# Values of a head multiplied one head later in the four short attention blocks of a hybrid decoder layer

## What is computed

```
h = rms_norm(x); proj = h @ w_in                      # q, k, v, indexer q/k/weights, four HGRN2 parts
for each block of 128 queries:                        # 16 blocks
    score = sum_h wi_h * relu(qi_h . ki)              # indexer, 8 heads of 64
    keep the 256 best causal keys of every query
    for each of 8 heads: p = softmax(q . k / 8 over kept keys); o = p @ v
hg  = gated linear recurrence (4 heads of 128)
x1  = x + rms_norm(concat(o, hg) @ w_out)
out = x1 + rms_norm((silu(n @ w_gate) * (n @ w_up)) @ w_down),  n = rms_norm(x1)
```

## Time and profile before

| | before |
|---|---|
| median of three runs | 3378.53 us |
| the profiled execution | 3383.49 us, span 3381.5 us |
| granted TensorE clock, mean | 0.983 |
| PE busy | 3214.6 us (95%) |
| DVE busy | 2267.9 us (67%) |
| ACT busy | 1501.5 us (44%) |
| DMA, mean | 102 GB/s |

### The profile page before, as it was taken

The page is one execution under the profiler, slowest core; times in us unless marked ns, Lnnn a source line. Parts: engine busy times, 40 slices in busy tenths (PEclk is TensorE's granted clock), DMA queues, the critical chain, the costliest instruction groups (busy, mean ns, idle before and its releaser), DMA issues.

```text
span 3381.5 us, 46512 instructions
## 1 busy us (share of the span) xinstructions
PE 3214.6 (95%) x18048; PEld 2836.7 (84%) x18048; DVE 2267.9 (67%) x3817; ACT 1501.5 (44%) x2477; POOL 237.1 (7%) x400
## 2 busy tenths in 40 slices
PE   8999999999888899999989999998999999989998
PEld 8999999998777788888778888887888888868886
DVE  3467777788565766666787777677876765463445
ACT  3454455445455454443554444445554444333222
POOL 0000000000111110010110001011000000010000
PEclk9999999999899999999989999999999999999999
DMA  5543443344222222222522212134111112252233
GB/s 182 168 134 121 131 149 125 114 139 130 98 84 104 94 83 80 68 85 69 180 83 76 71 63 79 64 111 150 63 65 60 64 52 74 95 182 97 91 105 107
DMA packets 147501, 345.66 MB, mean 102 GB/s; under 512 B 15057, under 2 KB 35921, under 8 KB 145233
## 3 DMA queue, kind: packets, MB, share of 16 engines
q1 hardware_dynamic: 144976, 338.49, 30.2%
q10 hardware_dynamic: 2304, 4.20, 0.3%
HBM read 283.31 MB, written 59.31 MB: 101 GB/s over the span
## 4 chain that ended last, share of the span: by engine, by line
PE 63%; DVE 5%; ACT 2%; issue 2%; DMA 1%; SPq 0%; DVEq 0%; POOL 0%; ACTq 0%; POOLq 0%
PE PJ_d L2069 9%; PE PJ_d L2071 9%; PE PJ_d L2070 9%; PE SC L2025 7%; PE PJ_d L2094 6%; PE PJ_d L2096 6%; PE PJ_d L2095 6%; PE SA L1984 3%; PE SA L2011 3%; PE SA L1985 3%; PE SA L1980 1%; DVE score L1716 1%; DVE wd_lo L1825 1%; DVE prob L1810 1%; DVE h_lo L1830 0%
## 5 line engine op out<-in xcount | busy, mean ns | idle before, releaser
L2069 PE MATMUL PJ_d<-h_hi,wd_hi 128*128 128x512 f32 (+1 forms) x1472 | 577.1, 392 | 15.4 <-DVE h_lo L1830 9.9
L2071 PE MATMUL PJ_d<-h_hi,wd_lo 128*128 128x512 f32 (+1 forms) x1472 | 564.6, 384 | 0.0
L2070 PE MATMUL PJ_d<-h_lo,wd_hi 128*128 128x512 f32 (+1 forms) x1472 | 563.8, 383 | 0.0
L1579 ACT ACTIVATE wd_hi<-wd_raw 128x512 fp32r<-128x512 f32 x568 | 345.2, 627 | 229.6 <-DMA wd_raw<-in_w_gu 128.6
L733 PE MATMUL PJ<-w_hi,h_hi 128*128 128x338 f32 (+1 forms) x1280 | 416.0, 325 | 2.8 <-DVE w_lo L550 2.8
L1825 DVE TENSOR_TENSOR wd_lo<-wd_raw,wd_hi 128x512 fp32r<-128x512 f32 x568 | 380.5, 689 | 45.9 <-ACT wd_hi L1579 42.9
L734 PE MATMUL PJ<-w_lo,h_hi 128*128 128x338 f32 (+1 forms) x1280 | 408.6, 319 | 0.0
L735 PE MATMUL PJ<-w_hi,h_lo 128*128 128x338 f32 (+1 forms) x1280 | 408.5, 319 | 0.0
L1574 ACT ACTIVATE pT<-SA 128x512 f32<-128x512 f32 (+3 forms) x320 | 156.6, 532 | 519.4 <-PE SA L2011 519.4
L1810 DVE CUSTOM_DVE_ANT_0 prob<-SA,bias 128x1024 f32<-128x1024 f32 (+7 forms) x192 | 170.1, 911 | 314.2 <-PE SA L1985 306.9
L2069 PEld LDWEIGHTS PJ_d<-h_hi,wd_hi 128*128 128x128 f32 x1472 | 280.8, 191 | 66.4 <-DVE wd_lo L1825 6.8
(11 more groups left out here) (207 smaller groups left out, 5724.6 us busy)
## 6 DMA issues: line engine op xcount, KB each, us to landing
wd_raw<-in_w_gu SPq DMA_DIRECT2D x352, 256.0 KB, 2.9
wd_raw<-in_w_down SPq DMA_DIRECT2D x176, 256.0 KB, 2.6
w_raw<-in_w_in SPq DMA_DIRECT2D x40, 684.0 KB, 4.6
w_raw<-in_w_in SPq DMA_DIRECT2D x40, 676.0 KB, 4.5
row_h<-proj_d SPq DMA_DIRECT2D x16, 1024.0 KB, 7.0
proj_d<-stage SPq DMA_DIRECT2D x40, 342.0 KB, 4.5
proj_d<-stage SPq DMA_DIRECT2D x40, 338.0 KB, 5.0
x_d<-acc SPq DMA_DIRECT2D x24, 512.0 KB, 2.9
```

The source lines that it names most:

```text
L1579: s_.activation(w_hi[:, u % RING, :], w_raw[:, u % RING, :], ACT.Copy).then_inc(w_hi_ready, 1)
L2069: t.matmul(to[:, tok], w_hi[:, r, w], h_hi[:, c, tok], start=(c == 0 and part != 1), stop=False)
L2070: t.matmul(to[:, tok], w_hi[:, r, w], h_lo[:, c, tok], start=False, stop=False)
L2071: last = t.matmul(to[:, tok], w_lo[:, r, w], h_hi[:, c, tok], start=False, stop=(c == KD - 1 and part != 0))
```

## The change

In the blocks with one chunk, PE multiplies the values of head h - 1 directly behind the turned probabilities of head h, ahead of slot B. The last head's values stay behind its slot B. In the other blocks nothing changes. Units 12 to 15, the `("out", 0, 0, 1, j)`, get the step 50 in place of 49, so that ACT rounds them in slot B of head 7 and the DVE splits them at step 51, in the index phase of block 4.

```diff
@@ -956,7 +956,8 @@
-        split_step[u] = min(max(freed + 2, split_step.get(u - 1, 0) + again), unit_first[u] - 3)
+        late = 1 if units[u][0] == "out" and units[u][1] == 0 and units[u][3] == 1 else 0
+        split_step[u] = min(max(freed + 2 + late, split_step.get(u - 1, 0) + again), unit_first[u] - 3 + late)
@@ -2122,6 +2123,14 @@
                     fill(("A", b, h))
+                    if NCH(b) == 1:
+                        turn_probs(b, h, 0)
+                        if h >= 1:
+                            values(b, h - 1, 0)
+                        fill(("B", b, h))
+                        if h == HEADS - 1:
+                            values(b, h, 0)
+                        continue
                     for p in range(pairs_of(b)):
```

## The result

The changed kernel takes 3362.9 us, the median of six runs (3360.6 to 3365.9), against 3379.3 (3376.7 to 3383.2) for the kernel before in the same job. The ratio is 0.9949, with a 95% interval of 0.9939 to 0.9959: 16.3 us less, where 19.9 were forecast. The profiled executions take 3365.1 and 3383.5 us, 18.4 apart.

The account below looks back on a forecast made before the run. PE, busy 95% of the span, was taken to bound the kernel. The terms 3.7 + 4.0 + 5.1 + 2.2 + 4.9 = 19.9 us, taken off the median of 3378.5, gave 3358.6 us; range 3353 to 3368.

Parts of the forecast that it names:

- The high ends: All parts of the change at their most favourable values: a total gain of about 24 us.
- The waits go, and PE's gain is kept: Blocks 0 to 3: waits for the copy fall from 13.0 to under 2 us; the DVE, behind PE, lets the gain stand.
- The rival that the softmax takes the copy's place: PE reaches the next turned head too soon and waits for its softmax, over 9 us in blocks 0 to 3; 3370.6; chance 0.10.
- Block 3, 3.7 us: Heads 2 to 5 of block 3: each gains 0.92 us by instruction starts, 3.7 in all; 2.8 by idle time.
- Block 2, 4.0 us: Heads 0 and 2 to 5 of block 2: five gaps of 0.80 us each go, 4.0 in all.
- Block 1, 5.1 us: Block 1: head 3 gives 3.8 us at full clock, head 4 0.3, head 6 0.7, head 7 0.3.
- the low branch: Block 1, head 3: if item 16 still runs at half clock, the gain is 1.5 us in place of 3.8.
- Block 0, 2.2 us: Block 0: 1.0 us from heads 0 to 2 and 1.2 from heads 3, 5, 6 and 7.
- Heads 0 to 2, taken as 1.0: Block 0, at half clock until about 914: gain between 0.7 and 2.3 us, taken as 1.0.
- The 1.2 us for heads 3, 5, 6 and 7: Block 0: the next softmax or an opening is close behind, so between 0 and 2.2 us, taken as 1.2.
- The split, 4.9 us: End of block 3 to item 52: head 7's softmax and item 52 come 5.0 us earlier, less 0.1 for ACT's roundings.
- Behind block 4 nothing changes: From block 4 on, all engines and loads are ahead by the same amount, and the rest takes as long as before.

Follow-up runs that it names:

- the last experiment: Against the changed kernel, the new order kept in blocks 2 and 3 alone, blocks 0 and 1 as before: 3368.9 us, ratio 0.9970.
- the second profile: Profile of the changed kernel run again with nothing changed, in a later job: 3362.3 us, ratio 0.9950.

## Why the prediction was right, and by how much not

Right were the sign, the mechanism and the range: 3362.9 against 3358.6 (3353 to 3368). The sum was 3.6 us too high, and the kernel before came out 0.7 above the median that it was taken from. The high ends as the prediction states them add up to 22.8 us, not to 24; with them the forecast's own lower bound would be 3355.7 and not 3354.5.

- **The waits go, and PE's gain is kept.** Under 2 us of waiting for the copy were forecast, 0.2 are left. The rival that the softmax takes the copy's place is refuted at its size, 4.3 us and not over 9. It is not wholly false: apart from head 7 of block 3, PE waits 2.3 us more for the softmax than before, 1.0 in block 0, 0.7 in block 1 and 0.5 in block 2.
- **Block 3, 3.7 us.** Measured 3.7, twice. Here the two ways to read the gap could be told apart: by starts 3.7, by the idle time of the row 2.8. The starts were right. That agrees with what the Trainium skill says in "Perfetto Trace Analysis", section "Tensor Engine Instruction", which the prediction weighed: the ends of matmuls are computed and not observed.
- **Block 2, 4.0 us.** Measured 3.9, twice. That it fits so well is in part luck. The five gaps gave 0.85 to 0.97 us each by starts, 4.45 in sum and not 4.0, and a new wait of 0.54 us for the softmax ahead of head 2, which the prediction did not see, took the excess back.
- **Block 1, 5.1 us.** Measured 3.0 and 3.1 (1.4 to 4.4, 1.4 to 4.5). The step that failed is the choice between 5.1 and 2.8, "nearer to the second": I compared the busy share of two stretches and took full clock. It fell in six of seven profiles with this order. The one that kept full clock gives 4.7 - 0.1 = 4.6 us, so the term would have been near right without the fall. For head 3 alone it would have been exact: from its turned probabilities to those of head 4 it takes 8.67 us before and 4.85 in that profile, 3.8 less, as forecast; with the fall it takes 6.47, which is 2.2 less, where the low branch had 1.5.
- **Block 0, 2.2 us.** Measured 1.4, with some 1 us of doubt, as the last experiment shows. Heads 0 to 2, taken as 1.0, gave 1.1: the lead at item 4 is 1.3 us, with the values of one head, 0.28 us, still to be done. The 1.2 us for heads 3, 5, 6 and 7 was the mistake: they gave 0.3, and under 0.1 in the second profile. Something else ends last behind them, as these rows after show (the first three are of heads 1 and 2, the others lie behind heads 3 and 6):

```profile
905.95 0.47 PE L2012 MATMUL SA<-ident,prob 128*128 128x128 f32 x1 [0.68 <-ACT prob L1563]
...
907.70 0.82 PE L1981 MATMUL SA<-ident,xt 128*64 128x128 f32 x3 [0.34 <-ACT pT L1575]
...
909.37 0.45 PE L2012 MATMUL SA<-ident,prob 128*128 128x128 f32 x1 [0.85 <-DVE nmx L1811]
...
915.68 0.33 PE L2012 MATMUL SA<-ident,prob 128*128 128x128 f32 x1 [0.35 <-ACT prob L1563]
...
925.68 1.03 PE L1981 MATMUL SA<-ident,xt 128*64 128x128 f32 x8 [0.71 <-DVE KT L1697]
```

The softmax, the copy (which an opening now waits for), the DVE's maximum and the DVE's part of the keys take the place of the copy ahead of the values. Of these, 1.0 us is the rival of the softmax.

- **The split, 4.9 us.** The chain was right: the softmax ahead of the roundings, the wait for it 5.66 - 0.61 = 5.05 us shorter where 5.0 were forecast, item 52 waits about 2 us for the subtractions (2.02), and what PE gains beyond that is lost there. The lead grows by 5.7 and 5.5 us up to item 52, more than forecast, and then item 52 gives 1.6 back where the clock falls in it, so that up to item 53 it is 4.0 and 5.4. I had named this wait and taken no fall behind it. By medians the units are worth 3.3 us, with an interval of the ratio from 0.9980 to 0.9998, 0.7 to 6.8 us; the size of this term is less sure than that of the order.
- **Behind block 4 nothing changes.** True of the code and, within 1.2 us in the two profiles of the changed kernel, of PE's idle time; single profiles still add 0 to 6 us, of which the clock explains the most.

In sum, at item 53: 1.4 + 3.0 + 3.9 + 3.7 + 4.0 to 5.4, which from the unrounded leads is 16.1 to 17.5, and the medians say 16.3. Of the 3.6 us that are missing 2.1 are block 1, of which 1.6 are its clock, and 0.8 block 0; the rest lies between the two readings of the split.

What stays open is what decides about a fall of the clock. It isn't the length of the idle time alone, as the runs show, and no run here moved anything else by itself. The theory that it depends on when the phase comes to the place fits the repeated profiles, but no run tested it.

## What to carry to other kernels

A wait of the bounding engine is priced from start to start of the instructions around it, and each place by itself: the gain is the gap up to what is late next, and in the shortest blocks something else is. Of a step that is moved, look at each engine's queue on its own: here ACT's part of the split gave all the gain, and the DVE's part, moved along with it, cost some of it and was better placed between two sums. Price a term whose waits stay at both levels of the clock, since here the idle time didn't tell which it would be. And don't believe a difference under some 6 us in 3400 from one profile of each kernel.

## What the hardware showed that was not expected

The same code, with the same idle time of PE ahead of the same matmuls, ran at half clock in one execution and at full clock in another: item 52 at 0.57 behind a wait of 2.02 us and at 1.00 behind 2.25 us, item 16 at full clock in one of seven profiles. It costs 1.4 to 1.6 us each time. From 1183 us to the end, where the code is the same, the lead over before grows by -0.2 to 6.2 us in eleven experiments and the changed kernel, with 44 to 72 us at half clock. In the changed kernel's two profiles, and in most others, less time at half clock goes with a larger lead. The granted clock in the profile's windows tells such stretches from a difference that the kernel makes.
